# Decay rows made once per tile for a gated delta rule on one core, with the order of work changed around them and around a feed-forward

## The chip, the cores and the metric

The kernel runs on one core of a Trainium2 chip. The metric is the device time of one launch in microseconds (us); the median of the runs is quoted, and the profiled execution has a time of its own. The engines are called PE (TensorE; PEld is its weight load), DVE (VectorE), ACT (ScalarE), POOL (GpSimd) and SP (SyncE, which here only issues DMAs).

## The reference

Two blocks run one after the other on 512 tokens of width 1024 (256 of the latent, 256 of the context) in float32. In the first block, layer 0 has an even mixer (attention and a gated linear attention) and layer 1 an odd mixer, the gated delta rule; each ends in a feed-forward with a squared ReLU. The second block has two layers of another kind and is not touched. What the change touches:

```python
h_lat = h_lat + ml[5] * sq_relu_mlp(modulate(rms_norm(h_lat, norm2_w[layer]), ml[3], ml[4]), ...)   # the context too
...
# gated delta rule, per head (8 heads, 64 by 128), both directions, chunks of 64 tokens
g = jnp.cumsum(log_a, axis=-1)
decay = jnp.where(incl, jnp.exp(g[..., :, None] - g[..., None, :]), 0.0)
a_mat = jnp.where(strict, einsum(kb, k) * decay, 0.0) + jnp.eye(C)
u, w = triangular_solve(a_mat, [v * beta, kb * jnp.exp(g)])
qk = einsum(q, k) * decay;  q_dec = q * jnp.exp(g)
def step(s, xs):
    v_new = u_c - w_c @ s
    o = qd_c @ s + qk_c @ v_new
    s = s * ge_c + ke_c.T @ v_new
```

## The kernel before

The whole program is one stream per engine, written out by hand; engines meet at semaphores, and each layer is a block of its own with a barrier of all engines at its end (L3835). Weights come in as "panels" of 128 by 2048 numbers: SP's queue loads three ahead (`raw`), ACT writes the rounded high part (`w_high`, L364) and DVE what is left (`w_low`, L372), into two buffers each. A weight product is three matmuls, low by high, high by high and high by low (L407, L408, L409). A plain f32 product is two instructions. While PE waits for a norm, `busy=(before, between, after)` gives it products of constants whose result nobody reads ("fillers", L972), and `busy_before` the same at the start of a layer.

**The feed-forward of layer 0** (`mlp0`, `feed_forward`) has 16 chunks. A chunk is an up product, `act_up` (L1203), `dve_up` (L1221), a high and a low part, and a down product of four groups of two banks. DVE adds every group to the sum y (`dve_add`, L1239). When the last chunk is added, `add_feed_forward` adds gate times y to x (L1400, 16 instructions), ACT squares x in eight blocks, PE sums them with a product by ones, ACT takes the root (L608), DVE the reciprocal (L641), which the split of a panel precedes, and layer 1 begins. Ahead of `mlp0` stands the norm `norm2_0`, whose last value `mlp_a_l` (L720) the up product of chunk 0 follows, pair of column blocks by pair.

**The odd mixer's first product** is `odd_g`: four panels, eight blocks of 128 rows. Block 0 takes the eight parts of the normed x (`a_l`, L773) as they come; blocks 1 to 7 and the narrow product `odd_ab_in` (128*32) follow.

**The rule** does four steps u (`STEPS`), each with a tile of 128 tokens (two chunks) for both directions d. A step's triangular matrix is inverted by doubling: PE's `t_products` (L2414) and `xy_products` (L2423, L2425), ACT's copies of T (L2570), and DVE's copies into X and Y (L2718, L2727), in levels n = 1 to 5, twice per level (a = 0, 1). In between, PE does what the step after needs, and the state's work of the step before. In order of PE's code at the end of step u:

- `row_sums(u + 1)` (L2365): the cumulated decays of each head, spread over all partitions. Each is a product of 128 by 128 by 128 with a column of `odd_log_a`: 16 products, 32 instructions.
- from these DVE's `differences` (L2693) makes E, and ACT the exponentials (L2561, L2564); `key_products` (L2379) and DVE's `decay_products` (L2705) make D of step u + 1, in one buffer. These wait for `corner_t` of step u, since D is read till then.
- `corner_first` (L2435), ACT's copy (L2623), `corner_second` (L2443): the quarter of the inverse that joins two chunks. DVE copies it into Yf (L2806), ACT copies the other quarters (`y_in_place`, L2584).
- `w_products` (L2456), `w_copy` on ACT (L2593, four copies of 64 partitions, each into its half of a zeroed buffer), `u_products` (L2467, L2469), DVE's `new_values` (L2736), `outputs` (L2479, L2481), `state_products` (L2492).

The rule's four heads on partitions 0 to 63 and four on 64 to 127 share tiles; what multiplies the state S has zeros in the other half, so its products contract 128 rows:

```python
nc.tensor.matmul(aux(d, r)[:, quarter(b)], w_t[d][:, r, b, :], S[:, d, b, :], start=False, stop=True)
```

## Time and profile before

| | |
|---|---|
| median of 3 runs | 2102.03 us (2099.11 to 2105.41) |
| the profiled execution | 2097.74 us, its span 2096.0 us |
| granted PE clock, mean | 0.984 of full |
| PE busy | 1990.2 us, 95% of the span |
| PE weight loads | 1747.4 us, 83% |
| DVE busy | 1533.1 us, 73% |
| ACT busy | 913.6 us, 44% |
| POOL busy | 140.5 us, 7% |
| DMA | 323.99 MB, mean 155 GB/s |

The places that the change touches lie between 353 us and 1108 us of the span: the start of `mlp0` at 353 to 375, its end at 700 to 739, `odd_g` at 739 to 774, the other projections of the odd mixer to 875, and the rule from 875 to about 1108. All else stays as it is, so the difference of the whole program is that of these places.

### The profile page before, as it was taken

To read this page: it belongs to the slowest core of one execution; us is meant where nothing else is said; L and a number is where in the kernel's file an instruction comes from. 1 tells how busy PE (TensorE), PEld (TensorE's weight loads), DVE (VectorE), ACT (ScalarE), POOL (GpSimd) and SP (SyncE) were. 2 spreads that over 40 slices of the span, in tenths; PEclk is the share of its full clock that TensorE was granted. 3 is DMA by queue.
4 is the path that set the end of the run, shared out by engine and by line. 5 is a ranking of instruction groups with operands and counts; after the bars stand their busy time and mean duration, and the time that the engine had idled before them with its cause. 6 is when DMAs were issued, how large, how long until landed. Compare 5 with 4: busy or idle time off the path is not lost. (4 is left out here: it accounts for less than half of the span.)

```text
span 2096.0 us, 40864 instructions
## 1 busy us (share of the span) xinstructions
PE 1990.2 (95%) x17088; PEld 1747.4 (83%) x17088; DVE 1533.1 (73%) x2430; ACT 913.6 (44%) x1379; POOL 140.5 (7%) x231
## 2 busy tenths in 40 slices
PE   7999999999999989988889999999999999999997
PEld 5787777888888768777888999889899978989997
DVE  6875648899776678765647777789777777967555
ACT  2445553222222243523326445556544455565443
POOL 0100000001010011111210010000000000000000
PEclk7999999999999999999999999999999999999999
DMA  8632014455454166300004677443467834424552
GB/s 333 205 138 99 1 42 140 142 194 200 169 195 182 60 253 224 110 4 3 4 3 176 246 279 270 156 162 121 141 232 275 280 136 161 141 101 141 184 184 93
DMA packets 59137, 323.99 MB, mean 155 GB/s; under 512 B 6384, under 2 KB 7536, under 8 KB 32624
## 3 DMA queue, kind: packets, MB, share of 16 engines
q1 hardware_dynamic: 33360, 228.97, 30.5%
q0 software_dynamic: 25344, 92.29, 12.4%
q8 instruction: 108, 1.77, 0.4%
q10 hardware_dynamic: 288, 0.66, 0.1%
q14 instruction: 37, 0.30, 0.0%
HBM read 320.84 MB, written 1.05 MB: 154 GB/s over the span
## 5 line engine op out<-in xcount | busy, mean ns | idle before, releaser
L372 DVE TENSOR_TENSOR w_low<-raw,w_high 128x1024 fp32r<-128x1024 f32 (+1 forms) x408 | 475.1, 1201 | 150.6 <-ACT w_high L364 150.2
L364 ACT ACTIVATE w_high<-raw 128x1024 fp32r<-128x1024 f32 (+1 forms) x408 | 402.8, 1034 | 333.7 <-PE banks L409 322.5
L550 DVE SCALAR_TENSOR_TENSOR mod_rows<-mod_rows,silu_condition 128x1024 f32<-128x1024 f32 x162 | 195.9, 1220 | 2.6 <-ACT silu_condition L453 1.0
L407 PE MATMUL banks<-ffn_pre_scaled_l,w_high 128*128 128x258 f32 x640 | 180.7, 282 | 0.4 <-DVE w_low L372 0.4
L409 PE MATMUL banks<-ffn_pre_scaled_h,w_low 128*128 128x258 f32 x640 | 180.6, 282 | 0.0
L408 PE MATMUL banks<-ffn_pre_scaled_h,w_high 128*128 128x258 f32 x640 | 180.4, 282 | 0.0
L409 PE MATMUL banks<-mlp_hidden_h,w_low 128*128 128x512 f32 (+1 forms) x512 | 173.2, 338 | 0.0
L408 PE MATMUL banks<-mlp_hidden_h,w_high 128*128 128x512 f32 (+1 forms) x512 | 173.1, 338 | 0.0
L407 PE MATMUL banks<-mlp_hidden_l,w_high 128*128 128x512 f32 (+1 forms) x512 | 173.1, 338 | 0.0
L536 POOL DMA_DIRECT2D mod_rows<-rows_dram x162 | 85.8, 530 | 1236.6 <-DVE mod_rows L550 1045.1
L407 PE MATMUL banks<-mix_l,w_high 128*128 128x256 f32 (+1 forms) x448 | 129.1, 288 | 3.4 <-DVE w_low L372 2.3
L408 PE MATMUL banks<-mix_h,w_high 128*128 128x256 f32 (+1 forms) x448 | 125.8, 281 | 0.0
L409 PE MATMUL banks<-mix_h,w_low 128*128 128x256 f32 (+1 forms) x448 | 125.8, 281 | 0.0
L407 PEld LDWEIGHTS banks<-ffn_pre_scaled_l,w_high 128*128 128x128 f32 x640 | 121.1, 189 | 0.8 <-DVE w_low L372 0.8
L408 PEld LDWEIGHTS banks<-ffn_pre_scaled_h,w_high 128*128 128x128 f32 x640 | 120.7, 189 | 0.0
L409 PEld LDWEIGHTS banks<-ffn_pre_scaled_h,w_low 128*128 128x128 f32 x640 | 120.2, 188 | 0.0
L408 PEld LDWEIGHTS banks<-mlp_hidden_h,w_high 128*128 128x128 f32 x512 | 96.1, 188 | 11.8
L407 PEld LDWEIGHTS banks<-mlp_hidden_l,w_high 128*128 128x128 f32 x512 | 96.2, 188 | 11.7
L409 PEld LDWEIGHTS banks<-mlp_hidden_h,w_low 128*128 128x128 f32 x512 | 96.1, 188 | 11.7
L407 PE MATMUL banks<-mlp_a_l,w_high 128*128 128x512 f32 x256 | 101.5, 397 | 0.0
L409 PE MATMUL banks<-mlp_a_h,w_low 128*128 128x512 f32 x256 | 101.1, 395 | 0.0
L408 PE MATMUL banks<-mlp_a_h,w_high 128*128 128x512 f32 x256 | 101.1, 395 | 0.0
(635 smaller groups left out, 5177.1 us busy)
## 6 DMA issues: line engine op xcount, KB each, us to landing
raw<-panels_dram SPq DMA_DIRECT2D x204, 1024.0 KB, 4.8
mod_rows<-rows_dram POOLq DMA_DIRECT2D x162, 512.0 KB, 5.2
mod_0a_rows<-rows_dram SPq DMA_DIRECT2D x8, 1024.0 KB, 19.4
odd_k_tok<-rows_dram POOLq DMA_DIRECT2D x14, 512.0 KB, 4.9
x_features<-x_features_dram SPq DMA_DIRECT2D x1, 2048.0 KB, 11.1
constants<-small_dram SPq DMA_DIRECT2D x1, 1672.5 KB, 6.7
silu_condition<-conditions_dram SPq DMA_DIRECT2D x2, 512.0 KB, 12.4
out_dram<-x_features SPq DMA_DIRECT2D x4, 256.0 KB, 2.1
```

Source lines behind the costliest of these rows:

```text
L364: self.nc.scalar.activation(self.wh[:, m % 2, cols], self.raw[:, slot, cols], ACT.Copy).then_inc(self.w_high, 1)
L372: self.nc.vector.tensor_tensor(self.wl[:, m % 2, cols], self.raw[:, slot, cols], self.wh[:, m % 2, cols].bitcast(F32), ALU.subtract).then_ ...
L407: self.nc.tensor.matmul(out, sh(k), ml(k), start=(opens and k == 0), stop=False)
L408: self.nc.tensor.matmul(out, sh(k), mh(k), start=False, stop=False)
L409: last = self.nc.tensor.matmul(out, sl(k), mh(k), start=False, stop=(closes and k == nk - 1))
L536: pool.dma_start(buffers[i % nb], self.rows[at, :, :]).then_inc(landed[i % nb], 16)
L550: nc.vector.scalar_tensor_tensor(row if v == nv - 1 else self.scratch[:], row, 1.0, self.cond[v][:], ALU.mult, ALU.mult, accum_out=mod[:, ...
```

## The change

**In the feed-forward of layer 0** (`direct`): in chunk 14 DVE adds gate times y to x already (`dve_begin_x`, 16 instructions), and the down products of chunks 14 and 15 go from PSUM straight to x (`dve_add_x`); ACT squares the blocks of x as they come, DVE adds four of them together, so PE sums five blocks, and two panels of layer 1 are split instead of one. The fillers of this norm are (0, 4, 2) instead of (2, 4, 2). `norm2_0` has 7 fillers between instead of 12, and its `gain` is followed without a semaphore of its own.

**In the odd mixer**: the first four blocks of `odd_g` take each part of x as it comes (`together=4`), so two of its panels have to be split ahead. `decay_rows` makes the decay sums as rows, once for all tiles: 16 products with 32 rows of result each, one after the other in the four row groups of a bank, and one ACT copy; `row_sums` then spreads a row over the partitions by a product that contracts 32 rows. D has two buffers. The corner's copy to Yf goes from DVE to ACT, ahead of `y_in_place`. `w_t`, `e_row` and `q_dec` lose their zero halves, and the products by them contract 64 rows; `w_copy` is two copies of 128 partitions. `u_products` and `outputs` take both directions in one, behind the waits of the second.

```diff
+        def to_x(src, q, v):
+            x = self.xT[:, q, v * direct["half"]:(v + 1) * direct["half"]]
+            gate = direct["mod"][:, direct["gate"] + q, v:v + 1]
+            return nc.vector.scalar_tensor_tensor(x, src[:, v * direct["half"]:(v + 1) * direct["half"]], gate, x,
+                                                  ALU.mult, ALU.add)
+        def dve_begin_x(dve):
+            for w in direct["gates"]:
+                dve.wait_ge(*w)
+            dve.wait_ge(y_ready, 4 * (chunks - 2))
+            for g in range(4):
+                for q in (2 * g, 2 * g + 1):
+                    for v in range(direct["nv"]):
+                        last = to_x(y[:, q, :], q, v)
+        def dve_add_x(dve, cs, q=None, groups=range(4)):
+            for g in groups:
+                dve.wait_ge(down_done, cs * 4 + (g + 1))
+                if cs == chunks - 1:
+                    dve.wait_ge(y_ready, cs * 4 + (g - 3))
+                for o in (2 * g, 2 * g + 1):
+                    for v in range(direct["nv"]):
+                        last = to_x(ps[:, 4 + o % 4, 0:n], o, v)
...
+                if direct is not None and which == "dve" and cs == chunks - 2:
+                    dve_begin_x(eng)
+                    add = dve_add_x
...
+            if direct is not None:
+                for g in range(4):
+                    dve_add_x(dve, chunks - 1, None, (g,))
+                    direct["between"](dve, g)
+            elif not keep:
...
-                        pr.copy_out(lambda q: gate[:, q, :]), a_ready, info=g_info, rising=True,
+                        pr.copy_out(lambda q: gate[:, q, :]), a_ready, info=g_info, rising=True, together=4,
...
+    sum_rows = y[:, 0:2, :].rearrange("p a (i n) -> p (a i) n", n=P)
+    def decay_rows(pe):
+        pe.wait_ge(beta_ready, 1)
+        for i in range(4):
+            for g in range(4):
+                last = nc.tensor.matmul(ps[32 * g:32 * g + 32, 7, i * P:(i + 1) * P],
+                                        la[:, min(i, 2):min(i, 2) + 2, :].rearrange("p i n -> p (i n)"), c("tri_b" if g >= 2 else "tri_f"),
+                                        start=True, stop=True)
+        last.then_inc(rows_done, 1)
+    def decay_rows_out(act):
+        act.wait_ge(rows_done, 1)
+        nc.scalar.activation(sum_rows, ps[:, 7, :].rearrange("p (i n) -> p i n", n=P), ACT.Copy).then_inc(rows_out, 1)
...
-    Dt = pr.sb("odd_D", [P, 2, H, P], ctx=t)
+    Dt = [pr.sb(f"odd_D_{i}", [P, 2, H, P], ctx=t) for i in range(2)]
...
-                i = tiles[d][u]
-                for r, b in paired:
-                    last = nc.tensor.matmul(aux(d, r)[:, quarter(b)],
-                                            la[:, i, 8 * d + 4 * r + b:8 * d + 4 * r + b + 1].broadcast_to([P, P]),
-                                            c("tri_b" if d else "tri_f"), start=True, stop=True)
-                last.then_inc(row_done, 1)
+            for b in range(4):
+                for d, r in four:
+                    if d in sides:
+                        g = 2 * d + r
+                        one = 36 * g + b + (16 if tiles[d][u] == 3 else 0)
+                        rows = slice(32 * g, 32 * g + 32)
+                        last = nc.tensor.matmul(aux(d, r)[:, quarter(b)], c("ident")[rows, one:one + 1].broadcast_to([32, P]),
+                                                sum_rows[rows, tiles[d][u], :], start=True, stop=True)
+            last.then_inc(row_done, len(sides))
...
         def u_products(u):
-            for d in range(2):
-                pe.wait_ge(w_out, each(u, d))
-                pe.wait_ge(s_ready, state(u, d))
-                i = tiles[d][u]
-                for r, b in paired:
+            pe.wait_ge(w_out, each(u, 1))
+            pe.wait_ge(s_ready, state(u, 1))
+            for b in range(4):
+                for d, r in four:
                     h = GDN_ORDER[4 * r + b]
                     nc.tensor.matmul(aux(d, r)[:, quarter(b)], Yf[:, d, 4 * r + b, :],
-                                     v_tok[:, i, h * P:(h + 1) * P], start=True, stop=False)
-                    last = nc.tensor.matmul(aux(d, r)[:, quarter(b)], w_t[d][:, r, b, :], S[:, d, b, :],
+                                     v_tok[:, tiles[d][u], h * P:(h + 1) * P], start=True, stop=False)
+                for d, r in four:
+                    last = nc.tensor.matmul(aux(d, r)[:, quarter(b)], w_t[halves[r], d, b, :], S[halves[r], d, b, :],
                                             start=False, stop=True)
-                last.then_inc(u_done, 1)
+            last.then_inc(u_done, 2)
         def outputs(u):
-            for d in range(2):
-                pe.wait_ge(vn_ready, each(u, d))
-                pe.wait_ge(qkt_ready, late(u, d))
-                pe.wait_ge(qd_ready, late(u, d))
-                for r, b in paired:
+            pe.wait_ge(vn_ready, each(u, 1))
+            pe.wait_ge(qkt_ready, late(u, 1))
+            pe.wait_ge(qd_ready, late(u, 1))
+            for b in range(4):
+                for d, r in four:
                     nc.tensor.matmul(aux(d, r)[:, quarter(b)], v_new[:, d, 4 * r + b, :], QKt[:, d, 4 * r + b, :],
                                      start=True, stop=False)
-                    last = nc.tensor.matmul(aux(d, r)[:, quarter(b)], S[:, d, b, :], q_dec[:, d, r, b, :],
+                for d, r in four:
+                    last = nc.tensor.matmul(aux(d, r)[:, quarter(b)], S[halves[r], d, b, :], q_dec[halves[r], d, b, :],
                                             start=False, stop=True)
-                last.then_inc(o_done, 1)
+            last.then_inc(o_done, 2)
...
+        def corner_in_place(u):
+            act.wait_ge(y_eye, 1)
+            act.wait_ge(corner_y, u + 1)
+            if u:
+                act.wait_ge(u_done, each(u - 1, 1))
+            for a, (j, i) in enumerate(corner_rows):
+                nc.scalar.activation(Yf[j, a, :, i], eight(ring["corner_y", u])[j], ACT.Copy).then_inc(corner_out, 1)
...
         def w_copy(u):
-            if u == 0:
-                act.wait_ge(zeroed, 2)
             for d in range(2):
                 act.wait_ge(w_done, each(u, d))
-                for r in range(2):
-                    last = nc.scalar.activation(w_t[d][halves[r], r],
-                                                aux(d, 0)[halves[r], :].rearrange("p (b n) -> p b n", n=P), ACT.Copy,
-                                                scale=-1.0)
-                last.then_inc(w_out, 1)
+                nc.scalar.activation(w_t[:, d], aux(d, 0).rearrange("p (b n) -> p b n", n=P), ACT.Copy,
+                                     scale=-1.0).then_inc(w_out, 1)
...
+            corner_in_place(u)
             y_in_place(u)
...
-                if u:
-                    dve.wait_ge(corner_t, u)
+                if u >= 2:
+                    dve.wait_ge(corner_t, u - 1)
                 for s in range(H):
-                    last = nc.vector.scalar_tensor_tensor(Dt[:, d, s, :], E[:, d, s, :],
+                    last = nc.vector.scalar_tensor_tensor(Dt[u % 2][:, d, s, :], E[:, d, s, :],
...
-            dve.wait_ge(corner_y, u + 1)
-            if u:
-                dve.wait_ge(u_done, each(u - 1, 1))
-            for a, (j, i) in enumerate(corner_rows):
-                nc.vector.tensor_copy(Yf[j, a, :, i], eight(ring["corner_y", u])[j]).then_inc(corner_out, 1)
...
                 a_ready = pr.norm_modulate("norm2_0", norm("norm2", 0), mod, nv, 24, 32, n, high, low,
                                            lambda k: [(ready[0][0], k + 1)], bank=0, scaled_x=y, work=squares,
-                                           busy=(0, 12, 1), begun=dict(scaled=scaled, squared=(squared, (folded, 5), [0, 6, 7])))
-                y, y_ready = pr.feed_forward("mlp0", D_FF // 256, False, n, high, low, a_ready, y, [], beside_mlp)
-                added = pr.add_feed_forward("mlp0", y, y_ready + outs[0], mod, 40, nv, n)
-                pr.next_norm(t, "norm1_1", n, lambda k: [(added[0][0], k + 1)], split=True, busy=(2, 4, 2))
+                                           busy=(0, 7, 1), begun=dict(scaled=scaled, squared=(squared, (folded, 5), [0, 6, 7])))
+                def add_next(dve, q):
+                    dve.wait_ge(next_squared, q + 1)
+                    if q > 1:
+                        dve.wait_ge(next_folded, q - 1)
+                    nc.vector.tensor_tensor(next_squares[:, 0, :], next_squares[:, 0, :], next_squares[:, q, :],
+                                            ALU.add).then_inc(next_folded, 1)
+                def between(dve, g):
+                    if g < 2:
+                        pr.split_dve(dve, pr.m, parts=(g,))
+                        pr.split_next["dve"] = pr.m + g
+                    if g:
+                        add_next(dve, g)
+                _, x_done = pr.feed_forward("mlp0", D_FF // 256, False, n, high, low, a_ready, y, [], beside_mlp,
+                                            direct=dict(mod=mod, gate=40, nv=nv, half=n // nv, gates=outs[0],
+                                                        between=between))
...
+                @pr.block.scalar
+                def _(act):
+                    pr.split_upto("act", act, pr.m)
+                    for q in range(KD):
+                        for w in x_done(q):
+                            act.wait_ge(*w)
+                        nc.scalar.activation(next_squares[:, q, :], pr.xT[:, q, 0:n], ACT.Square).then_inc(next_squared, 1)
+                pr.next_norm(t, "norm1_1", n, [], split=True, splits=1, squares=next_squares, busy=(0, 4, 2),
+                             squared=(next_squared, (next_folded, 3), [4, 5, 0, 6, 7]))
```

Three places in the engines' order. The first is DVE at the end of `mlp0`, from the last chunk but one to the reciprocal of the next norm. Before:

```order
L557 TENSOR_TENSOR mod_1<-mod_1,constants 128x32
L1221 SCALAR_TENSOR_TENSOR mlp_hidden<-banks,mlp_activated 128x1024
L1239 TENSOR_TENSOR mlp_y<-banks,mlp_y 128x1024
L1227 TENSOR_TENSOR mlp_hidden_l<-mlp_hidden,mlp_hidden_h 128x1024
L1239 TENSOR_TENSOR mlp_y<-banks,mlp_y 128x1024
L372 TENSOR_TENSOR w_low<-raw,w_high 128x1024 x2
L1239 TENSOR_TENSOR mlp_y<-banks,mlp_y 128x1024 x6
L1393 UNCONDITIONAL_BRANCH
L1400 SCALAR_TENSOR_TENSOR x_features<-mlp_y,mod_0,x_features 128x256 x16
L635 UNCONDITIONAL_BRANCH
L372 TENSOR_TENSOR w_low<-raw,w_high 128x1024 x2
L641 RECIPROCAL next_rstd<-norm_1_root 128x512
```

After:

```order
L1249 SCALAR_TENSOR_TENSOR x_features<-mlp_y,mod_0,x_features 128x256 x16
L1223 SCALAR_TENSOR_TENSOR mlp_hidden<-banks,mlp_activated 128x1024
L1249 SCALAR_TENSOR_TENSOR x_features<-banks,mod_0,x_features 128x256 x4
L1229 TENSOR_TENSOR mlp_hidden_l<-mlp_hidden,mlp_hidden_h 128x1024
L1249 SCALAR_TENSOR_TENSOR x_features<-banks,mod_0,x_features 128x256 x4
L372 TENSOR_TENSOR w_low<-raw,w_high 128x1024 x2
L1249 SCALAR_TENSOR_TENSOR x_features<-banks,mod_0,x_features 128x256 x12
L372 TENSOR_TENSOR w_low<-raw,w_high 128x1024
L1249 SCALAR_TENSOR_TENSOR x_features<-banks,mod_0,x_features 128x256 x4
L372 TENSOR_TENSOR w_low<-raw,w_high 128x1024
L3737 TENSOR_TENSOR norm_1_squares<-norm_1_squares 128x512
L1249 SCALAR_TENSOR_TENSOR x_features<-banks,mod_0,x_features 128x256 x4
```

The additions to x (L1400, behind the last chunk) stand ahead of the last chunk's own work as the x16 row of L1249, and each group of down products adds to x itself; behind row L3737 shown last, one more group, two more of L3737, two splits (L372) and the reciprocal (L641) follow.

The second is ACT at the end of the rule's first step and in the second's start: the last decays' exponentials, the corner, Y in place, and w. Before:

```order
L2564 ACTIVATE odd_E<-odd_E 128x1024 x2
L2623 ACTIVATE odd_T<-banks 128x512
L2575 ACTIVATE odd_X<-constants 128x1024
L2584 ACTIVATE odd_Yf<-odd_Y 64x8x64 x4
L2570 ACTIVATE odd_T<-banks 128x512 x2
L2593 ACTIVATE mod_rows<-banks 64x512 x4
```

After:

```order
L2633 ACTIVATE odd_E<-odd_E 128x1024 x2
L2695 ACTIVATE odd_T<-banks 128x512
L2644 ACTIVATE odd_X<-constants 128x1024
L2662 ACTIVATE odd_Yf<-banks 64x8x64 x2
L2653 ACTIVATE odd_Yf<-odd_Y 64x8x64 x4
L2639 ACTIVATE odd_T<-banks 128x512 x2
L2667 ACTIVATE mod_rows<-banks 128x512 x2
```

Two corner copies (L2662) stand ahead of `y_in_place`, and w is copied in two instructions instead of four.

The third is PE in `u_products` of the first step. Before, 16 pairs like these two:

```order
L2467 MATMUL banks<-odd_v_tok,odd_Yf 128x128
L2469 MATMUL banks<-odd_S,mod_rows 128x128
L2467 MATMUL banks<-odd_v_tok,odd_Yf 128x128
L2469 MATMUL banks<-odd_S,mod_rows 128x128
L2467 MATMUL banks<-odd_v_tok,odd_Yf 128x128
```

After, the whole of it:

```order
L2534 MATMUL banks<-odd_v_tok,odd_Yf 128x128 x4
L2537 MATMUL banks<-odd_S,mod_rows 128x128 x4
L2534 MATMUL banks<-odd_v_tok,odd_Yf 128x128 x4
L2537 MATMUL banks<-odd_S,mod_rows 128x128 x4
L2534 MATMUL banks<-odd_v_tok,odd_Yf 128x128 x4
L2537 MATMUL banks<-odd_S,mod_rows 128x128 x4
L2534 MATMUL banks<-odd_v_tok,odd_Yf 128x128 x4
L2537 MATMUL banks<-odd_S,mod_rows 128x128 x4
```

Products with the full 128 rows and products with 64 rows now alternate in groups of four, eight phases in all, over both directions (L2534 is the old L2467, L2537 the old L2469).

## Rows read from the trace of the kernel before

**Rows 1.** Windows: us, busy time of PE, PEld, DVE, ACT, POOL, clock, DMA share, GB/s.

```profile
780.00:875.00 95.00, 94.98 (x428) 76.94 (x429) 76.92 (x114) 34.56 (x52) 10.55 (x20) 1.00 0.58 197
...
875.00:1120.00 245.00, 210.17 (x5599) 190.95 (x5598) 142.96 (x300) 89.44 (x132) 44.75 (x51) 0.98 0.04 12
...
738.76:745.44 6.68, 6.67 (x10) 2.84 (x11) 5.47 (x11) 5.16 (x11) 2.08 (x4) 0.55 0.87 319
```


**Rows 2.** Timeline, mlp0's start: start us, us, engine line operation [idle before, releaser].

```profile
353.17 10.46 PE L972 MATMUL banks<-constants 128*128 128x512 f32 x24
...
368.67 0.88 DVE L720 SCALAR_TENSOR_TENSOR mlp_a_l<-mlp_y,mod,mlp_a_h 128x256 fp32r<-128x256 f32 x2 [0.19 <-ACT mlp_a_h L736]
...
374.87 1.03 ACT L1203 ACTIVATE mlp_activated<-banks 128x1024 f32<-128x1024 f32 x1 [6.23 <-PE banks L409]
```


**Rows 3.** Timeline of DVE and ACT at mlp0's end.

```profile
700.73 1.22 DVE L1221 SCALAR_TENSOR_TENSOR mlp_hidden<-banks,mlp_activated 128x1024 f32<-128x1024 f32 x1 [6.25 <-ACT mlp_activated L1203]
...
722.07 1.22 DVE L1239 TENSOR_TENSOR mlp_y<-banks,mlp_y 128x1024 f32<-128x1024 f32 x1 [1.57 <-PE banks L409]
...
723.33 6.42 DVE L1400 SCALAR_TENSOR_TENSOR x_features<-mlp_y,mod,x_features 128x256 f32<-128x256 f32 x16
...
732.22 0.66 ACT L608 ACTIVATE norm_root<-banks,constants 128x512 f32<-128x512 f32 x1
...
733.67 3.35 DVE L641 RECIPROCAL next_rstd<-norm_root 128x512 f32<-128x512 f32 x1
```


**Rows 4.** Timeline of PE and DVE at layer 1's start, in odd_g.

```profile
738.76 6.68 PE L972 MATMUL banks<-constants 128*128 128x512 f32 x8 [3.27 <-PEq L3835]
...
762.30 0.28 PE L407 MATMUL banks<-a_l,w_high 128*128 128x256 f32 x1
...
773.56 0.40 PE L407 MATMUL banks<-a_l,w_high 128*32 128x512 f32 x1
...
750.56 1.43 DVE L773 TENSOR_TENSOR a_l<-odd_v_tok,a_h 128x512 fp32r<-128x512 f32 x2
...
752.24 2.36 DVE L372 TENSOR_TENSOR w_low<-raw,w_high 128x1024 fp32r<-128x1024 f32 x2 [0.26 <-ACT w_high L364]
```


**Rows 5.** Timeline of PE, products of full and of 64 rows.

```profile
261.26 1.16 PE L1680 MATMUL banks<-gla_att,even_gv 128*128 128x128 f32 x8
...
262.35 0.44 PE L1686 MATMUL banks<-even_y 64*128 64x64 f32 x4
...
926.26 2.06 PE L2379 MATMUL banks<-odd_kT 64*128 64x128 f32 x32
...
967.60 3.84 PE L2365 MATMUL banks<-constants,odd_log_a 128*128 128x128 f32 x32
```


**Rows 6.** Timeline of DVE and ACT where step 1 ends and 2 begins.

```profile
969.69 4.23 DVE L2693 TENSOR_SCALAR odd_E<-banks,odd_g_sum 128x128 f32<-128x128 f32 x16 [1.25 <-PE banks L2365]
...
980.01 4.22 DVE L2705 SCALAR_TENSOR_TENSOR odd_D<-odd_E,odd_minus_beta,banks 128x128 f32<-128x128 f32 x16 [3.00 <-PE banks L2435]
...
984.15 1.40 DVE L2806 COPY odd_Yf<-banks 64x512 f32<-64x512 f32 x2
...
987.84 0.60 ACT L2570 ACTIVATE odd_T<-banks 128x512 f32<-128x512 f32 x1 [3.80 <-PE banks L2414]
```


**Rows 7.** Timeline at the rule's tail: ACT, PE and DVE in step 3.

```profile
1087.95 2.56 ACT L2584 ACTIVATE odd_Yf<-odd_Y 64x512 f32<-64x512 f32 x4
...
1090.84 1.97 PE L2456 MATMUL banks<-odd_Yf,odd_keg 128*64 128x128 f32 x32 [1.71 <-DVE odd_Yf L2806]
...
1091.97 2.41 ACT L2593 ACTIVATE mod_rows<-banks 64x512 f32<-64x512 f32 x4 [1.46 <-PE banks L2456]
...
1093.21 0.49 PE L2467 MATMUL banks<-odd_v_tok,odd_Yf 128*128 128x128 f32 x2 [0.41 <-ACT mod_rows L2593]
...
1100.66 1.23 DVE L2736 TENSOR_TENSOR odd_v_new<-banks,odd_beta 128x1024 f32<-128x1024 f32 x1 [2.35 <-PE banks L2469]
...
1107.81 1.06 ACT L364 ACTIVATE w_high<-raw 128x1024 fp32r<-128x1024 f32 x1 [1.10 <-PE banks L2481]
```

More of the change, by code:

```diff
@@ L1240, in dve_add @@
                 ins.then_inc(y_ready, 1)
+        x_final = self.sem(f"{name}_x_final") if direct is not None else None
+        def to_x(src, q, v):
[11 more added lines that the diff above has]
+                        last = to_x(y[:, q, :], q, v)
+            self.dve_chain.then(dve, last)
+        def dve_add_x(dve, cs, q=None, groups=range(4)):
[6 more added lines that the diff above has]
+                        last = to_x(ps[:, 4 + o % 4, 0:n], o, v)
+                    if o % 2:
+                        last.then_inc(y_ready, 1)
+                    elif cs == chunks - 1:
+                        last.then_inc(x_final, 1)
         def turn(body, eng):
@@ L1258, in feed_forward, with step @@
         early = deferred is not None and gated
-        def step(which, up, high_or_low, add, rows=lambda eng, point: None):
+        def step(which, up, high_or_low, add_to, rows=lambda eng, point: None):
             def body(eng, cs, q):
+                add = add_to
                 if within and which == "dve" and q is None and cs == chunks - 2:
@@ L2228, in beside_qk @@
             decay_sums(eng)
+            decay_rows(eng)
+        if which == "act" and p == 2:
+            decay_rows_out(eng)
         if which == "dve" and p == 2:
@@ L2301, in odd_mixer @@
     paired = [(r, b) for b in range(4) for r in range(2)]
+    four = [(d, r) for d in range(2) for r in range(2)]
     each = lambda u, d: 2 * u + d + 1
@@ L2667, in _ @@
         y_identity(0)
-        for d in range(2):
-            nc.gpsimd.memset(w_t[d], 0.0)
-            nc.gpsimd.memset(e_row[d], 0.0).then_inc(zeroed, 1)
         pool.wait_ge(eg_ready, 3)
```

57 lines of the change are left out of this document (29 added, 28 removed).

## The prediction

> **What bounds the kernel now.** I read the windows first, to see stage by stage whether PE or a chain sets the time, and then the timeline at each edited place. PE alone is the bound from 780 to 875 us: it is busy for 94.98 of 95.00 [rows 1], and there an added PE instruction costs its own time. In the rule, 875 to 1120, PE shows 210.17 of 245.00, DVE 142.96 and ACT 89.44, with hardly any DMA (share 0.04) [rows 1]; no engine is full, so the chain from PE to ACT to DVE and back sets the time, and only what lies on it counts. At the start of mlp0, at its end and in odd_g the question is who waits for whom, and the rows are read at those places. The places stand behind one another in time and none covers another, so their savings add up. All times are against the profiled execution's own 2097.74 us, which is 4.3 below the median of 2102.03; I add 4.3 at the end.
>
> **Start of mlp0: -3.6.** The 24 filler instructions begin at 353.17 and hold PE until 363.63 (0.436 each), though the normed x comes in pairs of blocks whose last ends at 368.67 + 0.88 = 369.55 [rows 2]. ACT takes the first up product at 374.87 [rows 2]. A block of odd_g, 24 products with 256 columns, takes (773.56 - 762.30)/4 = 2.815 us [rows 4], so one takes 0.117, and one with 512 columns 0.235. The first up product has 48 of these, 11.3 us, and 363.63 + 11.3 = 374.9: PE worked without a pause and the fillers' end set the time. With 14 instructions the fillers end at 353.17 + 6.1 = 359.3, and 11.3 later is 370.6; now the last part of x decides, 369.55 + 6 x 0.235 + 0.2 = 371.2. That is 3.6 less (3 to 4).
>
> **End of mlp0: -5.7.** Before, the last down group ends just before 722.07; DVE adds it (1.22), adds gate times y to x (723.33 to 729.75), ACT squares, PE sums, the root starts at 732.22 (0.66), the reciprocal at 733.67, behind two splits, and takes 3.35; fillers of the next layer start at 738.76, 1.7 behind it [rows 3, 4]. After, the last group is four instructions of 6.42/16 = 0.40, so x is final at 723.75; one add of squares, then PE's three last blocks (two instructions of 0.436 each) end at 727.05, the root at 727.8, and the splits (2.4 behind 724.45) are over by then. Reciprocal to 731.3, barrier to 733.0, against 738.76. The 16 early additions, 6.4 us, are not free by themselves: they lie in DVE's idle 6.25 us ahead of 700.73 [rows 3], and at most 0.3 is left over. Without that cover they would cost their 6.4 and the edit would bring nothing. Of the x additions nothing else is late; range -3 to -7.
>
> **odd_g: -2.4.** PE starts layer 1 with fillers until 738.76 + 6.68 = 745.44, the last pair of x parts ends at 750.56 + 1.43 = 751.99, and block 4 begins at 762.30 [rows 4]. So four blocks took 16.9 us of which 11.3 are PE work: block 0 waited part by part. With four blocks side by side there is work from the first part on, 745.44 + 11.3 = 756.7, past the last part. But both weight buffers are held until then, and the third panel is split only after: ACT's high part some 1.06 (as in [rows 7]) before DVE's low part of two instructions (2.36 [rows 4]), of which I take 3.2 with the wait. Blocks 4 to 7 then run from 759.9 to 771.2, against 773.56. The bounds are 0 (the split is later still) and -5.6 (no gap).
>
> **decay_rows: +1.3.** 16 f32 products, 32 instructions with 128 columns, in the stretch where PE is full. Full-size ones take 3.84 for 32 [rows 5]; ones in two row groups at a time 2.06 [rows 5], 0.54 of it. In four groups I take half of that again, 1.03, and 0.3 for the start and the change of shape. Bounds 1.0 and 3.8. The ACT copy lies in ACT's idle share (34.56 of 95 busy [rows 1]).
>
> **The rule's three step boundaries: -15.6.** Before, at the one shown [rows 5, 6]: row sums 967.60, differences 969.69 to 973.92, four copies of X and Y, decay products only at 980.01 after 3.00 idle behind the corner's first product, then the corner copies 1.40, then X and Y again, so that ACT copies T of direction 0 at 987.84. After: the row sums are 16 products on 32 rows, 1.03 by the reckoning above, and both directions are done when they end; differences start at 968.65 (-1.04), the 3.00 idle goes since D has a second buffer, and the 1.40 goes from DVE. DVE alone would be 5.44 earlier. ACT has now the corner as well, 2 x 0.6 (0.60 each as in [rows 6]), ahead of Y in place (2.56, as in [rows 7]); walking through its queue (exponentials; T 0.60; X, a copy as large as the 1.06 of [rows 7]; corner 1.2; Y 2.56) it comes to T at 983.0, 4.85 earlier. The second direction is 5.45 earlier. I take 5.2, three times. It is 3 each if ACT's corner copies wait longer.
>
> **Inside the steps: -1.4, -1.2, +0.9.** w_copy is two copies of 0.6 instead of four, 2.41 [rows 7]; u_products now wait for both, so I count 0.5 per step of the three inner ones. The u block took (1100.66 - 0.1) - 1093.21 = 7.35 [rows 7]. The new one has four full phases of 8 instructions, each 262.35 - 261.26 = 1.09 with the change of shape [rows 5], and four phases of 8 instructions on 64 rows, 8 x 2.06/32 = 0.52 plus 0.12: in all 6.9, so -0.4 three times. The outputs of step 2 wait for the second direction's v_new: +0.9 in net. Here the row groups are bought with changes of shape: by the full phase, 8 x 0.115 = 0.92 would be without, and 1.09 is with, 0.17.
>
> The Trainium skill, TensorEngine Tiling (Array Packing), Tiling Modes, says that changing the tiling mode drains TensorE. The trace agrees, 0.17 us by the phase above. The Trainium skill, TensorE: Matmul & The Clock Gate, Part 3, gives 3.07 times the speed for four row groups of 32; by that page the row sums would be an estimated 3.84/3.07 = 1.25 and the sum 0.7 less.
>
> **The tail: +5.9.** In the last step nothing hides. Before, DVE's corner copies, which release w at 1090.84, ran beside ACT's Y in place, 1087.95 to 1090.5, and w's copies start at 1091.97, u at 1093.21 [rows 7]. After, ACT does the corner copies first and Y in place behind them, and u waits for both copies of w: u starts about 1094.75, +1.5. Both directions of u end at 1101.7, DVE makes both v_new one after the other, 2 x 1.23, to 1104.2 (before, one of them and its outputs lay under the other), outputs take 6.9 to 1111.15, and the copy and squares of direction 0, before hidden, follow: ACT gets to its panel at 1113.75 against 1107.81. Range +3 to +8.
>
> **Sum.** -3.6 - 5.7 - 2.4 + 1.3 - 15.6 - 1.4 - 1.2 + 0.9 + 5.9 = -21.8: an execution of 2075.9, a median of 2080. Taken alone the likeliest case spans 2073 to 2088.
>
> **Rivals.**
> *Changes of shape and row groups cost more.* If a pair of phases costs 0.35 more, six u and output blocks with four pairs each give back 8.4; if four row groups do no better than two (2.06 [rows 5]), the boundaries lose 1.1 each, and decay_rows is 3.8. That leaves -7.6, a median of 2094. For it: shapes change eight times in each block. Against it: the 1.09 and 2.06 measured. Chance 0.07.
> *ACT becomes the bound of the boundaries.* It gets the corner copies and stands then in the way of T; if it saves 3 and not 5.2 each, the sum is -15.2, 2087. For it: ACT's queue is in fixed order and X in DVE comes earlier than ACT is free; against it, its idle 3.80 ahead of 987.84 [rows 6]. 0.10.
> *The gain at mlp0's end is lost,* since the early additions delay the hidden part of chunk 15, or the barrier waits for something else: -16.1, 2086. 0.05.
> *The clock is better at layer 1's start.* In 738.76 to 745.44 the granted clock is 0.55 and 8 fillers take 6.68 against 0.436 each elsewhere [rows 1, 2, 4]; with less idle PE ahead of it they would take 3.5: 3.2 more, a median of 2077. 0.13.
> *Slower: the clock falls more in the rule.* With less PE work in the rule and a new gap in odd_g, PE may be granted the lower of its two levels more often. The clock there is 0.98 [rows 1], some 10 us at half rate of 245. At half rate PE work doubles, as the fillers show; 3.4 us of it cost about 1.5. To cancel 21.8 takes some 50 us more at half rate, a mean clock of about 0.88. That gives over 2108. Against it: the edits at the boundaries make PE's gaps shorter, not longer. 0.04.
>
> The Trainium skill, TensorE: Matmul & The Clock Gate, Part 1, says that an idle TensorE is set to the lower of two clocks. The trace agrees at 738.76, where the low stretch follows a wait of PE; by that rule the shorter wait there and the longer one in the tail pull to either side.
>
> **How the numbers follow.** The forecast has 0.61, the rivals 0.07, 0.10, 0.05, 0.13, 0.04. A change of 0.3%, 6.3 us, is about what a measurement of this kernel can tell from none, so same means 2095.7 to 2108.3: 0.04, the upper part of the first rival and of mixtures; slower 0.04; faster 0.92. The range 2069 to 2092 leaves out most of the first rival and the last, and at the low end a better clock together with odd_g's gap gone.
>
> **What will show it.** The first up product is taken by ACT at 371.2; fillers of layer 1 begin near 729.4 (733.0 less the 3.6 from before); odd_g's block 4 starts some 3.2 behind block 3's end; 32-row products 1.0 to 1.3 for a step's 32 instructions; DVE's 3.00 idle before the decay products is gone; a boundary 5.2 shorter; in the tail w and u later and outputs in one block. I am wrong if a u block takes more than 8 us, if ACT stands between DVE's X and the next T by more than 2 us, or if PE's clock in the rule is under 0.95.

## The result

The changed kernel takes 2086.16 us (median of 6 runs, 2081.80 to 2090.69), the kernel before, over the 6 runs beside it, 2100.11. The ratio is 0.9929 with a 95% interval of 0.9912 to 0.9946: 14.9 us faster by the ratio (11.3 to 18.5) and 13.95 by the medians, where 21.8 had been forecast, a median of 2080. The profiled execution of the changed kernel takes 2086.92, span 2085.1, against a span of 2096.0. The runs of the changed kernel lie further apart than those before, and they follow the clock: 2081.8 at a mean granted clock of 0.985 and 2082.0 at 0.986, 2085.4 at 0.984, 2086.9 at 0.982, 2088.8 and 2090.7 at 0.981.

The two spans differ by 10.9. Laid side by side at the same places of the program, the difference came about like this (differences of start times of like instructions; negative is time saved, us):

| stretch | forecast | measured |
|---|---|---|
| start of mlp0, to ACT's first up product | -3.6 | -3.2 |
| end of mlp0, to layer 1's fillers | -5.7 | -5.4 |
| odd_g, to the narrow product | -2.4 | -3.6 |
| decay rows, to the rule's first product | +1.3 | +1.1 |
| the rule's steps, to ACT's last copy of T | -17.3 | -12.4 |
| tail, from there to ACT's panel (L364) | +5.9 | +11.4 |
| the rest of the program | 0 | +1.0 |

**Up to the rule** the forecast's steps can be read one by one. In time order, from the timeline of the changed kernel, the rows that answer to [rows 2], [rows 3] and [rows 4], with decay_rows (L2214) last (start us, us, engine, line, operation, idle before):

```profile
353.14 6.17 PE L972 MATMUL banks<-constants 128*128 128x512 f32 x14
371.69 1.03 ACT L1205 ACTIVATE mlp_activated<-banks 128x1024 f32<-128x1024 f32 x1 [3.08 <-PE banks L409]
...
691.21 6.42 DVE L1249 SCALAR_TENSOR_TENSOR x_features<-mlp_y,mod,x_features 128x256 f32<-128x256 f32 x16
...
719.21 1.66 DVE L1249 SCALAR_TENSOR_TENSOR x_features<-banks,mod,x_features 128x256 f32<-128x256 f32 x4
...
724.40 0.69 ACT L608 ACTIVATE norm_root<-banks,constants 128x512 f32<-128x512 f32 x1 [0.97 <-PE banks L630]
...
749.96 0.39 PE L407 MATMUL banks<-a_l,w_high 128*128 128x256 f32 x1 [3.11 <-DVE w_low L372]
...
761.46 0.39 PE L407 MATMUL banks<-a_l,w_high 128*32 128x512 f32 x1
...
826.33 1.08 PE L2214 MATMUL banks<-constants,odd_log_a 128*32 128x128 f32 x32
```

The fillers end at 359.31 and ACT has the up product at 371.69 (371.2 forecast). The x additions of chunk 14 lie in DVE's idle time, the last group of the last chunk is 1.66 instead of 1.22 + 6.42, and the root starts 5.2 after its begin, not 10.2 [rows 3]. The gap that was forecast behind odd_g's four common blocks is 3.11 (3.2 forecast), and decay_rows takes 1.08.

**A boundary of steps**, the same one as in [rows 5, 6], DVE first and ACT behind it, with PE's row sums (L2434) ahead:

```profile
951.07 1.17 PE L2434 MATMUL banks<-odd_y,constants 32*128 32x128 f32 x32
...
952.40 4.20 DVE L2761 TENSOR_SCALAR odd_E<-banks,odd_g_sum 128x128 f32<-128x128 f32 x16
...
958.96 4.20 DVE L2773 SCALAR_TENSOR_TENSOR odd_D<-odd_E,odd_minus_beta,banks 128x128 f32<-128x128 f32 x16
...
962.66 1.21 ACT L2662 ACTIVATE odd_Yf<-banks 64x512 f32<-64x512 f32 x2 [0.35 <-issue]
963.89 2.56 ACT L2653 ACTIVATE odd_Yf<-odd_Y 64x512 f32<-64x512 f32 x4
966.48 0.60 ACT L2639 ACTIVATE odd_T<-banks 128x512 f32<-128x512 f32 x1
```

Row sums take 1.17 instead of 3.84, where 1.03 was forecast. By the factor of 3.07 in the Trainium skill, TensorE: Matmul & The Clock Gate, Part 3, they would take an estimated 1.25; here the factor is 3.3. From the start of the differences to ACT's copy of T it is 14.08 now and was 18.15: the 3.00 idle ahead of the decay products is gone. ACT's walk ends right at the copy of T, as forecast.

**The tail**, PE from w to the outputs, with DVE's new values between:

```profile
1068.51 3.27 PE L2524 MATMUL banks<-odd_Yf,odd_keg 128*64 128x128 f32 x32 [2.70 <-ACT odd_Yf L2653]
...
1081.22 2.36 DVE L2804 TENSOR_TENSOR odd_v_new<-banks,odd_beta 128x1024 f32<-128x1024 f32 x2 [18.54 <-PE banks L2537]
...
1083.63 2.07 PE L2547 MATMUL banks<-odd_QKt,odd_v_new 128*128 128x128 f32 x8 [2.46 <-DVE odd_v_new L2804]
1085.63 1.23 PE L2550 MATMUL banks<-odd_q_dec,odd_S 64*128 64x128 f32 x8
...
1089.95 1.16 PE L2547 MATMUL banks<-odd_QKt,odd_v_new 128*128 128x128 f32 x8
1091.04 0.71 PE L2550 MATMUL banks<-odd_q_dec,odd_S 64*128 64x128 f32 x8
```

The same instructions take 2.07 and 1.23 at first and 1.16 and 0.71 four groups later; w takes 3.27 where it took 1.97 [rows 7]. The windows of the tail, before's and the changed kernel's (columns as in [rows 1]), say why:

```profile
1087.33:1107.81 20.48, 17.71 (x193) 17.36 (x194) 6.40 (x7) 6.62 (x11) 1.12 (x2) 1.00 0.16 53
```

```profile
1064.01:1095.91 31.90, 23.22 (x193) 19.66 (x194) 4.63 (x5) 6.54 (x11) 1.12 (x2) 0.79 0.10 34
```

The granted clock is 0.79 instead of 1.00: PE spent two stretches, some 13.6 us by the windows microsecond by microsecond, at the lower of its two levels (1.2 instead of 2.4 GHz). The first begins at 1069.4, while w runs, behind the wait of 2.70 for it; the second at 1083.1, near the end of the wait of 2.46 for the new values.

**The three boundaries** can be measured like the one above, from the first row sum to ACT's first copy of T in the next step. They took 20.35, 20.24 and 21.68 and take 15.71, 15.41 and 16.85: 14.3 less in all, of 15.6 forecast. Another 1.5 of the 12.4 lie ahead of ACT's very first copy of T. From the first product with D it is 4.20 there now and was 5.66, and a low stretch of the clock stood in it before (granted 0.70 for 893.11 to 898.77, 1.00 now). So the rest of the steps became 3.4 longer, where 1.7 less was forecast. From ACT's first copy of T to its last, before and after, each with two low stretches of 3.4 us:

```profile
898.77:1087.33 188.56, 161.63 (x5120) 153.74 (x5114) 110.45 (x236) 56.71 (x88) 32.98 (x36) 0.98 0.02 4
```

```profile
886.35:1064.01 177.66, 152.93 (x5120) 141.36 (x5118) 106.34 (x231) 57.21 (x87) 27.89 (x32) 0.98 0.02 4
```

**Inside the steps** something else stands. PE's waits, before and after, over the steps and the tail (total us, times, longest):

```profile
PE banks L2402 <- DVE odd_Yf L2806: 6.9, 3, 2.3
...
PE banks L2423 <- issue: 3.5, 4, 1.5
...
PE banks L2414 <- issue: 2.2, 3, 1.3
PE banks L2425 <- issue: 2.1, 3, 1.4
```

```profile
PE banks L2493 <- issue: 7.3, 7, 1.8
PE banks L2491 <- issue: 3.0, 5, 1.2
PE banks L2482 <- issue: 3.0, 4, 1.6
```

The 6.9 us that PE waited for D behind DVE's corner copies are gone (1.6 behind ACT's, L2470, stand in their place), but waits that nothing in the profile releases ("issue") at the levels' products (L2482, L2491, L2493; before L2414, L2423, L2425) grew from 7.8 to 13.3. Where do they stand? Count all of PE's records from the start of the program (matmuls, weight loads and the semaphore and control records between them) and divide by 256: nearly all of these waits stand in front of a record with remainder 198. (Matmuls and weight loads alone do not give one remainder.) A count of PE's pauses over 0.1 us, times in which it has neither a matmul nor a weight load, from the rule's first product with D to the last outputs:

| kernel | pauses at remainder 198 | other pauses |
|---|---|---|
| before | 14, 10.8 us | 20, 19.5 us |
| changed | 20, 15.2 us | 15, 16.6 us |

One pause in each row's first column is an ordinary wait that falls there by chance (0.68 for ACT's T, 0.48 for Yf); without them it is 13 with 10.1 us and 19 with 14.7. And the stream of instructions itself is to be seen as DMA packets (queue 8, 16 KB each). From 896 to 945 us, before and after:

```profile
q8 instruction: 12, 0.20, 1.6%
```

```profile
q8 instruction: 13, 0.21, 1.9%
```

That is one packet every 3.8 us in the changed kernel, at the densest every 3.3. From the first product with D to ACT's last copy of T there are 41 packets and 41.6 times 256 records, before and after. In both traces no block begins sooner than 1.2 us behind the end of a packet, and at each of the 13 and 19 pauses PE goes on 1.2 to 1.5 us behind one. So PE gets its instructions in blocks of 256, and where it wants the next one sooner it pauses up to 1.8 us. The Trainium skill, Advanced Engine Details and Errata, ISA Cache, says that a cache line holds 256 instructions in 16 KB; the traces agree, with 16,384 bytes a packet and the pauses multiples of 256 records apart. The forecast had not looked at this.

The pauses are not all of it. Outside the boundaries they grew by 2.9. There PE also waits longer ahead of the third row sums for QKt (1.97, before 0.85) and ahead of the state products for y (1.45, before 0.42), 2.1 more. Together that is the size of what is missing in the steps, 5.1; that each lies on the chain was not shown.

### The profile page after: what moved, and what is told of

Its sections match the earlier page's. It is cut to its first block and busy times, and to the rows that moved or that the text cites. A ratio compares the mean times of both kernels' runs of the same rounds, so it can differ in the third digit from the quotient of the medians.

```text
span 2085.1 us, 40897 instructions
## 1 busy us (share of the span) xinstructions
PE 1976.3 (95%) x17100; PEld 1731.0 (83%) x17100; DVE 1532.1 (73%) x2449; ACT 914.6 (44%) x1380; POOL 132.3 (6%) x223
## 5 line engine op out<-in xcount | busy, mean ns | idle before, releaser
L372 DVE TENSOR_TENSOR w_low<-raw,w_high 128x1024 fp32r<-128x1024 f32 (+1 forms) x408 | 475.1, 1200 | 147.8 <-ACT w_high L364 147.3
L364 ACT ACTIVATE w_high<-raw 128x1024 fp32r<-128x1024 f32 (+1 forms) x408 | 402.7, 1034 | 339.2 <-PE banks L409 329.3
## 6 DMA issues: line engine op xcount, KB each, us to landing
silu_condition<-conditions_dram SPq DMA_DIRECT2D x2, 512.0 KB, 12.4
```

What stands on the lines that cost most here:

```text
L364: self.nc.scalar.activation(self.wh[:, m % 2, cols], self.raw[:, slot, cols], ACT.Copy).then_inc(self.w_high, 1)
L372: self.nc.vector.tensor_tensor(self.wl[:, m % 2, cols], self.raw[:, slot, cols], self.wh[:, m % 2, cols].bitcast(F32), ALU.subtract).then_ ...
```

## The experiments

Two theories came out of the traces. **Clock:** the tail's new waits put PE at its lower level, and that is what made the tail 5.5 longer than forecast. **Supply:** in the steps, PE's instruction supply takes back part of what the removed waits gave.

**e1_abc and e2_rule**: the change in two. The first has everything outside the rule (both ends of mlp0, odd_g), the second the rule alone.

> The rule as before; only the start of mlp0, its end and odd_g are changed. By the forecast's terms 3.6 + 5.7 + 2.4 = 11.7 less than before, some 2088. The traces of before and after show the rule's start 10.96 earlier and the end of the program 10.9 earlier, so if the rule's part is worth nothing on the median too, this kernel is as fast as the changed one, 2086 to 2089. If the profile after only fell on an unlucky clock and the rule's part is worth its 11, the changed kernel would have to be at 2077 and this one lies 2 behind its 2086.

> Only the rule is changed (decay rows, two buffers of D, corner copies on ACT, half products, both directions in one). Forecast's terms: -15.6 -1.4 -1.2 +0.9 +5.9 +1.3 = -10.1, 2090. Theory of the clock (the new waits in the tail put TensorE at its lower level and give the gain back): about -1, 2099, with a tail (from ACT's last copy of T to the next panel's split) of 31 to 32 us and granted clock below 0.7 in it. Rival, structure alone: the tail is just as long without a low clock.

Measured: e1_abc 2084.98, ratio 0.9925 (0.9911 to 0.9940); e2_rule 2099.72, ratio 0.9988 (0.9976 to 1.0000), both against 2100.45. What is outside the rule gives 15.8 us (12.6 to 18.7), the rule's rewrite 2.5 (0 to 5). The tail of e2_rule is 32.3 with this window:

```profile
1077.05:1109.31 32.26, 23.73 (x193) 20.60 (x194) 4.63 (x5) 6.54 (x11) 1.13 (x2) 0.73 0.10 33
```

A clock of 0.73 (below 0.7 was expected), so this is not the accident of one trace: the tails of e6, e7 and e11, which have the same work, take 31.8, 30.8 and 33.3 with 13.6 us or more at the lower level. Its steps, from the first copy of T to the last, take 175.46 against 188.56 before: the gain is there and the tail eats it. This profiled execution is the slowest of twelve that lie between 2092.3 and 2103.0.

**e3_tail_fill**: products of constants in PE's three waits of the tail.

```diff
+        pr.keep_busy(pe, 3, free)
         w_products(STEPS - 1)
+        pr.keep_busy(pe, 1, free)
         u_products(STEPS - 1)
+        pr.keep_busy(pe, 3, free)
         outputs(STEPS - 1)
```

> The changed kernel with products of constants in TensorE's three waits of the tail (3 before w, 1 before u, 3 before outputs). Clock theory: TensorE stays at the full level, w takes 2.0 instead of 3.3, u 7.0 instead of 8.7, outputs 7.0 instead of 9.9, so the tail goes from 31.9 to 26.4 and the kernel is 4 to 6 faster than the changed one, 2081. Rival, the tail is long by its waits: the same 31.9 or a little more, since fillers run on past the waits' ends, 2086 to 2088.

Measured: 2083.46, ratio 0.9918 (0.9904 to 0.9931), 2.7 below the changed kernel's median, on another chip; the intervals of the two overlap, so the runs alone don't tell them apart. The tail:

```profile
1061.49:1088.10 26.61, 23.71 (x207) 17.51 (x208) 4.63 (x5) 6.54 (x11) 1.13 (x2) 1.00 0.11 41
```

26.6 at a clock of 1.00, where the clock theory had 26.4. The same work in the same order was 5.3 shorter, with more work in it. The tail's structure costs 26.6 - 20.5 = 6.1, the forecast's 5.9, and the clock the rest. The median moved less than expected (4 to 6), and the execution with this trace, 2079.02, is the fastest of the five; that low stretches elsewhere made the others longer is likely and not shown.

**e4_tail_dir**: in the last step u and outputs go direction by direction again.

```diff
-        u_products(STEPS - 1)
-        outputs(STEPS - 1)
+        u_products_by_direction(STEPS - 1)
+        outputs_by_direction(STEPS - 1)
```

> The changed kernel, but in the last step u and outputs go direction by direction, each behind its own waits. Structure theory: v_new and outputs of direction 0 lie again under direction 1, so new values (1.2), the copy and squares of direction 0 (2.6) and part of the wait for w come off, -4 to -5 without help of the clock, 2081.5. Clock theory: the wait ahead of the outputs (2.46) goes too, so the low stretch at the outputs disappears and the tail is 9 shorter, 2077 to 2079. Against both: eight more changes of shape, +0.8.

Measured: 2082.37, ratio 0.9911 (0.9897 to 0.9926), 3.8 below the changed kernel's median with intervals that overlap; 2081.5 or 2077 to 2079 was expected.

```profile
1063.58:1088.91 25.33, 21.85 (x193) 17.18 (x194) 5.03 (x6) 6.63 (x12) 1.12 (x2) 0.93 0.11 43
```

The tail went from 31.9 to 25.3, 6.6 shorter, of which the clock (0.93 instead of 0.79) is a part; between both theories. One low stretch stays, behind the wait of 2.7 for w.

**e5_corner_dve**: the corner copies on DVE again, D still in two buffers.

> The changed kernel, with the corner copies back on VectorE behind the decay products, D still in two buffers. Forecast's reasoning: the copies cost VectorE 1.4 in each of three boundaries ahead of X and Y, and ACT's queue is 1.2 shorter, so each boundary is about 1 longer; the tail gets 1.3 back, since they run beside Y in place. In all +1 to +3 against the changed kernel, 2087 to 2089. Rival (ACT had become the bound at the boundaries): each boundary 1 shorter and the tail too, -4, 2082.

Measured: 2084.76, ratio 0.9923 (0.9910 to 0.9936): no difference from the changed kernel that the runs can tell, where 1 to 3 more was expected. The steps, at a clock of 1.00, take:

```profile
886.74:1064.27 177.53, 149.55 (x5120) 138.05 (x5119) 110.04 (x237) 53.66 (x81) 27.87 (x32) 1.00 0.02 4
```

against those of e3_tail_fill, also at 1.00, where ACT does the copies:

```profile
887.64:1061.49 173.85, 149.62 (x5120) 138.42 (x5118) 106.29 (x231) 57.16 (x87) 27.86 (x32) 1.00 0.02 4
```

That is 3.7 longer, but not at the boundaries. From the corner's copy of T to the next T of direction 0 they take 5.90, 6.06 and 5.97 against 5.84, 5.71 and 5.71, 0.7 more in all. 2.4 of the 3.7 are pauses at remainder 198 (16.9 against 14.5). So the corner copies cost about the same on either engine. The rival fails too, since no boundary became shorter without ACT's copies. The tail is 26.6 instead of 31.9, with a clock of 0.92 instead of 0.79: most of that is the clock.

**e6_full_rows**: no decay rows; row sums with 128 rows in each step.

> The changed kernel, but the decay sums' rows aren't made and each step's row sums are 128-row products again (32 instructions, 3.84). Forecast: decay_rows' 1.2 comes off, each boundary loses 1.0 for direction 0 of the differences and about 0 for direction 1 up to 2.8 where TensorE itself is next, so +2 to +5, 2088 to 2091. Rival (TensorE's instruction supply sets the pace there): the rows' saving lies in time that the supply takes anyway, and the kernel is as fast as the changed one or 1 faster.

Measured: 2088.65, ratio 0.9946 (0.9933 to 0.9959), 2.5 over the changed kernel by the medians, though the two intervals overlap. The steps take 181.3 instead of 177.7, and the three boundaries, from the first row sum to the next T, 17.33, 18.02 and 17.98, together 5.4 more, so the saving of the short products shows in the trace; +2 to +5 was expected.

**e7_shift**: 116 more instructions ahead of the rule, to move the blocks' edges.

```diff
-                pr.keep_busy(pe, 3, 3)
+                for _ in range(32):
+                    nc.tensor.matmul(ps[0:32, 3, 0:64], c("ones")[:, 0:32], pr.cst[:, 0:64], start=True, stop=True)
```

> The changed kernel, with 32 small products of constants (128 instructions with their weight loads) in place of 3 fillers (12) ahead of the keys' turning, so 116 more instructions ahead of the rule's steps. In the traces so far every pause of TensorE that nothing releases stands at a multiple of 256 instructions (matmuls and weight loads counted together, remainder 198). Theory of the instruction supply: they stay at remainder 198 of the count, which is now 116 instructions earlier in the code, some 7 to 12 pauses, together 12 to 16 us. Rival (they belong to certain products, such as where X is written): they stay at the same products and the remainder moves to 314 - 256 = 58.

Measured (one run, 2086.05): 17 pauses at remainder 198, 16.1 us, more of them than the 7 to 12 expected, and at 58 a single one of 0.49, the ordinary wait for Yf. They stand at other products than in the changed kernel (one now at the row sums) and at the same count, all of PE's records taken. So they belong to the count and not to the code.

**e8_half_levels**: only four of eight heads in the products of the levels; the rest of the inverse is left out.

> The changed kernel, with only half the heads in the products for T, X and Y of the inverse's levels; the other half of the inverse is left out. Supply theory: half the instructions in the same chain of ACT and VectorE copies; the pauses at every 256th instruction shrink from 14.5 us to under 3, on top of the products' own 1.0 per group. Rival (the pauses are waits for semaphores or PSUM, one or two per level): they stay at 10 or more.

Measured (one run): 2054.24; 3 pauses at remainder 198 or the record beside it, 1.0 us in all, where the changed kernel has 15.2, and 0.70 of the 1.0 is the ordinary wait for T. The other pauses grew from 16.6 to about 30: PE now waits for ACT and DVE at each level. The packets in the same window, 9 instead of 13:

```profile
q8 instruction: 9, 0.15, 1.4%
```

With fewer instructions in the same chain the supply keeps up. That is what the supply theory says; waits for semaphores or PSUM would have stayed.

**e9_best**: e4_tail_dir, and in the last step the corner copies on DVE beside ACT's Y in place, and one product of constants ahead of w.

```diff
+            if u + 1 < STEPS:
                 corner_in_place(u)
...
+        pr.keep_busy(pe, 1, free)
         w_products(STEPS - 1)
         u_products_by_direction(STEPS - 1)
```

> The changed kernel; in the last step u and outputs go direction by direction, the corner copies of that step go to VectorE beside ScalarE's Y in place, and one product of constants stands ahead of w. Against the kernel with the directions apart (tail 25.3, of it 3.4 at the low clock) 1.3 for the corner and 1.5 for the clock: a tail of 22.5 and 2079 to 2081, some 5 under the changed kernel. Rival (the clock falls just the same): 2082, as with the directions alone.

Measured: 2076.67 (2074.41 to 2080.46), ratio 0.9889 (0.9872 to 0.9907), 24.7 below before and 9.5 below the changed kernel (8.4 by the ratios; the intervals lie apart) and below the 2079 to 2081 expected. The tail is 22.5 at 1.00, as expected:

```profile
1063.54:1086.08 22.54, 21.23 (x195) 16.34 (x196) 6.40 (x8) 5.45 (x10) 1.13 (x2) 1.00 0.15 48
```

**e10_abc_fill**: e1_abc with two products of constants ahead of w.

> The kernel with the rule as before, with two products of constants ahead of the tail's w. Clock theory: its tail (22.3, with 6.8 us at the low clock) goes back to the 20.5 of the kernel before, -2, 2083. Rival (the low stretch there follows the sparse work of the levels, not the wait): the same 2085.

Measured: 2085.19, ratio 0.9921 (0.9906 to 0.9937), the same as e1_abc. Its tail does go back from 22.34 (clock 0.85) to 20.62 (1.00), as the clock theory has it, but in this execution the low stretches in the steps add up to 13.6 us instead of 10.2, and the steps take 188.5 instead of 186.4. So the rival was right on the median and wrong on the mechanism: the low stretch did follow the wait. The profiled execution is the slowest of its six. Filling this one wait did not show on the median.

**e11_no_together**: odd_g's first four blocks one after the other as before.

> The changed kernel, but odd_g's first four blocks go one after the other as before. Forecast's term: +2.4 (0 to 5.6) against the changed kernel, 2088.5; the first narrow product then starts 2.4 to 3.6 later behind the layer's start. Rival (what was gained there is given back in the rule's instruction supply or its clock): 2086, though odd_g ends later.

Measured: 2090.39, ratio 0.9949 (0.9935 to 0.9963), 4.2 over the changed kernel (the intervals overlap a little): more than the 2.4 of the forecast, in its range. The narrow product starts 35.79 behind the layer's first filler instead of 31.24, 4.55 later, where 2.4 to 3.6 was expected. PE waits again for four parts of x, 0.8 to 0.9 each, and a low stretch of 6.8 us begins in the last of these waits (granted 0.57 from 743 to 751), some 3 of the 4.55.

## Why the prediction was right, and where not

The direction, the range and the order of size were right; 21.8 was forecast and 14 to 15 measured. The forecast of 2080 also stands on a median of three, 2102.03, that is 2100.11 with the three later runs. Two rivals, at 2086 and 2087, name the measured time, but neither of their mechanisms came: that they fit is luck. By the forecast's steps:

- **Start of mlp0, end of mlp0, decay_rows**: right to 0.4 each in the trace.
- **odd_g**: the mechanism with its gap of 3.1 was right; the term was 2.4 and measured 3.6 in the trace and 4.2 as a kernel of its own (e11). 1.3 of the 3.6 is the clock: 8 fillers take 5.37 instead of 6.68, the rival "the clock is better at layer 1's start", which came in for less than half. And the forecast read the 5.6 that the four blocks lost before as waits alone. Some 1.6 of them were a low stretch behind these waits (752 to 755, weight products 0.21 apart instead of 0.12), and the changed kernel, without the waits, has none there. So more of this term than the forecast says is clock, as in e11.
- **The three boundaries** (-15.6): 14.3 less, 4.6 to 4.8 each. The mechanism and the size were right: the waits named went, and ACT ended its walk as it was counted.
- **Inside the steps** (-1.4 - 1.2 + 0.9 = -1.7): 3.4 more. The 1.5 won ahead of the very first copy of T are left out of this; a low stretch had cost them before, which is luck. These are the terms that failed, by 5.1. They took PE to be ready for what came. In its place the traces show 2.9 more of pauses at the edges of instruction blocks here (over the whole rule 10.1 became 14.7) and 2.1 more in two waits, for QKt and y. e7 and e8 tie the pauses to the count of instructions. How much a removed wait brings back as such a pause is open: with the rule as before, e1_abc has 6.8 us of them and before 10.1, and its steps are 2.2 shorter. Two slips are small: three times 0.5 is 1.5 and not 1.4, and the 0.115 for a full product stands in no row; 3.84/32 = 0.12 gives 0.13 for the change of shape instead of 0.17.
- **The tail** (+5.9): its structure was right, 6.1 at the full clock (e3). What failed is the tacit step that the tail's PE work would run at the full level. It forecast the later starts of w, u and the outputs, behind which PE waits (2.70 and 2.46), and priced none of the clock that they bring; measured 5.3 more. The rival "slower: the clock falls more in the rule" had the mechanism, but priced it only where it cancels the whole gain, some 50 us at half rate. It came as 13.6 us at half rate in the tail. The sentence against it, that the edits make PE's gaps shorter, held for the boundaries and not for the tail.
- **Changes of shape** (a rival at 0.07): the pairs of phases take 1.73 (1.16 and 0.71 less overlaps, from 1089.95 to 1091.68), as forecast. It did not come.
- **ACT as the bound of the boundaries** (0.10): the copy of T starts the moment that ACT's walk ends (966.45 and 966.48 above), so ACT does set it, but where the forecast had counted it, 4.8 earlier and not 3. Without the corner copies (e5) it comes no sooner.
- **The signs of being wrong**: a u block over 8 us came, 8.7 in the tail at the low clock (1072.46 to 1081.17), 6.9 with the fillers at the full clock (e3). The clock in the rule, 0.95 from the first product with D to the last outputs, is on the edge. ACT stood less than 2 us between X and T.

That the rule's rewrite taken alone is worth some 2.5 (e2) says that most of the change's 14.9 come from both ends of mlp0 and odd_g; the gain in the steps, 11 to 13, is about what the tail lost, 11 to 12.

## What to carry to other kernels

When two interleaved halves are merged to save PE work, look at the last step, where nothing covers them: split there (e4; with the corner copies beside Y and one filler, e9, -9.5). Price each new wait of PE in a stretch of small products twice, for itself and for the clock of what follows. And in a stretch with many small products, count PE's instructions per microsecond before counting a removed wait as won: here a block of 256 came no faster than every 3.3 us.

## What was not expected of the hardware

- PE's instructions came in packets of 16,384 bytes, 256 instructions; in the rule they started 3.3 us apart at the least and 3.9 in the median, a block began 1.2 us behind its packet at the soonest, and PE paused 0.2 to 1.8 us at such edges, 10.1 us in all before and 14.7 after.
- In the tail PE fell to the lower level after waits of 2.7 and 2.5 amid small products; small f32 products then took 2.07 instead of 1.16 (128 rows) and 1.23 instead of 0.71 (64 rows).
- Products on 32 rows in four row groups took 1.17 for 32 instructions, on 64 rows 2.06, on 128 rows 3.84.
- The runs of the changed kernel differ by up to 9 us with the mean granted clock (0.981 to 0.986), those of e2_rule by 10.7 (0.978 to 0.985).
